# RWKV-7 recurrence: some products on the other two 64x64 tiles, copies moved between engines, and a new order of steps

## What is computed

```python
def _wkv7_scan(S0, r, w, k, v, kk, a):
    def step(S, inp):
        r_t, w_t, k_t, v_t, kk_t, a_t = inp
        sa = jnp.einsum("bhvk,bhk->bhv", S, -kk_t)
        S = (S * w_t[:, :, None, :] + sa[..., None] * (kk_t * a_t)[:, :, None, :]
             + v_t[..., None] * k_t[:, :, None, :])
        o_t = jnp.einsum("bhvk,bhk->bhv", S, r_t)
        return S, o_t
...
    kk = kk / jnp.maximum(jnp.sqrt(jnp.sum(kk * kk, axis=-1, keepdims=True)), 1e-12)
...
    mean = jnp.mean(o, axis=-1, keepdims=True)
    var = jnp.mean(jnp.square(o - mean), axis=-1, keepdims=True)
    o = ((o - mean) * lax.rsqrt(var + LNX_EPS) * lnx_g + lnx_b)
    o = o + jnp.sum(r * k * r_k, axis=-1, keepdims=True) * v
    o = o.reshape(B, T, D) * jax.nn.silu(g)
    return o @ w_o, h[:, -1], S
```

## Time and profile before

| | us |
|---|---|
| median of 3 runs | 1933.91 |
| lowest, highest | 1926.66, 1935.87 |
| the profiled execution | 1932.09 |
| its span, first to last instruction | 1930.1 |
| PE busy | 1802.9 (93%) |
| DVE busy | 1049.6 (54%) |
| ACT busy | 798.0 (41%) |
| POOL busy | 249.6 (13%) |

### The profile page before, as it was taken

One profiled execution on the slowest core, in us unless ns is written; L12 is line 12 of the kernel. 1 busy time (PEld: TensorE's weight loads), 2 busy tenths in 40 slices (PEclk: granted clock), 3 DMA queues, 4 the chain that ended last, 5 costly groups with the idle time before them and its releaser, 6 DMA issues.

```text
span 1930.1 us, 43901 instructions
## 1 busy us (share of the span) xinstructions
PE 1802.9 (93%) x18432; PEld 1538.8 (80%) x18432; DVE 1049.6 (54%) x1718; ACT 798.0 (41%) x1459; POOL 249.6 (13%) x315
## 2 busy tenths in 40 slices
PE   7999999999999999999998998999999998778797
PEld 6988999999888888799986776777776776334697
DVE  6744464453588999444445533443463445676334
ACT  4234233233466767333333323233343444555233
POOL 0300000000245555232000000000000001010032
PEclk9999999999999999999999999999999999998899
DMA  8534554555355553243889999999999999999541
GB/s 295 185 142 156 179 180 155 170 179 165 92 137 139 142 137 97 92 141 143 340 292 417 420 419 409 414 426 425 426 426 417 414 425 380 418 393 364 211 146 71
DMA packets 154200, 510.45 MB, mean 264 GB/s; under 512 B 60097, under 2 KB 81986, under 8 KB 108738
## 3 DMA queue, kind: packets, MB, share of 16 engines
q1 hardware_dynamic: 153442, 503.66, 68.8%
q10 hardware_dynamic: 576, 4.19, 0.6%
HBM read 472.86 MB, written 32.32 MB: 262 GB/s over the span
## 4 chain that ended last, share of the span: by engine, by line
PE 31%; DMA 19%; DVE 3%; ACT 2%; issue 2%; SPq 1%; DVEq 0%; ACTq 0%
DMA at_vraw<-in_cache_v 19%; PE psP L2648 8%; PE psP L2650 7%; PE psP L2649 7%; PE at_psO L2702 5%; PE at_psS L2681 3%; SPq L2061 1%; PE psP L2747 0%; DVE wlo L2410 0%; SPq L2101 0%; PE at_psT L2693 0%; DVE at_w L2498 0%; ACT at_p_w L2368 0%; DVE at_p_rc L2593 0%; ACT at_p_w L2366 0%
## 5 line engine op out<-in xcount | busy, mean ns | idle before, releaser
L2648 PE MATMUL psP<-xhi,whi 128*128 128x320 f32 x1488 | 475.3, 319 | 2.9 <-DVE xlo L2535 1.9
L2650 PE MATMUL psP<-xhi,wlo 128*128 128x320 f32 x1488 | 460.7, 310 | 0.0
L2649 PE MATMUL psP<-xlo,whi 128*128 128x320 f32 x1488 | 460.5, 309 | 0.0
L2648 PEld LDWEIGHTS psP<-xhi,whi 128*128 128x128 f32 x1488 | 280.2, 188 | 64.9 <-issue 63.4
L2410 DVE TENSOR_TENSOR wlo<-wraw,whi 128x2048 fp32r<-128x2048 f32 x92 | 212.9, 2314 | 207.7 <-ACT whi L2236 207.5
L2236 ACT ACTIVATE whi<-wraw 128x2048 fp32r<-128x2048 f32 x92 | 176.0, 1913 | 276.7 <-PE psP L2650 275.5
L2649 PEld LDWEIGHTS psP<-xlo,whi 128*128 128x128 f32 x1488 | 280.5, 189 | 0.1
L2650 PEld LDWEIGHTS psP<-xhi,wlo 128*128 128x128 f32 x1488 | 280.3, 188 | 0.0
L139 PE MATMUL psP<-xhi,whi 128*128 128x320 f32 x704 | 218.1, 310 | 2.7 <-DVE wlo L174 2.3
L140 PE MATMUL psP<-xlo,whi 128*128 128x320 f32 x704 | 217.6, 309 | 0.0
L141 PE MATMUL psP<-xhi,wlo 128*128 128x320 f32 x704 | 217.5, 309 | 0.0
(11 more groups left out here) (382 smaller groups left out, 3075.5 us busy)
## 6 DMA issues: line engine op xcount, KB each, us to landing
wraw<-in_weights SPq DMA_DIRECT2D x156, 1024.0 KB, 5.9
at_kraw<-in_cache_k SPq DMA_DIRECT2D x96, 1024.0 KB, 11.1
at_vraw<-in_cache_v SPq DMA_DIRECT2D x94, 1024.0 KB, 10.9
at_kraw<-in_cache_k SPq DMA_DIRECT2D x64, 512.0 KB, 9.8
at_vraw<-in_cache_v SPq DMA_DIRECT2D x62, 512.0 KB, 10.7
rw_s0t<-in_s0T SPq DMA_DIRECT2D x16, 256.0 KB, 3.7
o_wkv_s<-rw_SN SPq DMA_DIRECT2D x16, 256.0 KB, 3.1
wraw<-in_weights ACTq DMA_DIRECT2D x4, 1024.0 KB, 6.5
```

What stands on the lines that cost most here:

```text
L2648: pe.matmul(out, wh, c_.xhi[:, kc, :], start=(kc == 0), stop=False)
L2649: pe.matmul(out, wh, c_.xlo[:, kc, :], start=False, stop=False)
L2650: last = pe.matmul(out, wl, c_.xhi[:, kc, :], start=False, stop=(kc == NM - 1))
```

## The change

Three products move to the two cross tiles: `ss`, `var`, and in `AB` the products with KZ. A cross tile takes rows of one head and writes to the partitions of the other, so `sq` and `csq` are written with their halves exchanged (two ACT instructions of 64 partitions each in place of one of 128; the sum brings the halves back), and `KK` is read from PSUM with exchanged halves (two DVE instructions of 64 partitions). The copies of SA0 to SA3 go from DVE to ACT, and xl from DVE to POOL. `ORDER` is a new list. The semaphore of the moved blocks is split in two, for B and for K, and in every tile `S0` now waits for both; before, it did so only in the last.

```diff
-LATE = set("""... R.g.y R.a.xh R.v.xl P.t.Ht P.a.Ht
+LATE = set("""... R.g.y R.a.xh R.g.xl P.t.Ht P.a.Ht
...
-STILL_READ = {"s4": "v.D4s", "X": "v.X", "S3": "v.ST3", "mean": "v.cen", "O0": "a.O0", "O1": "a.O1", "SN": "v.SNa"}
+STILL_READ = {"s4": "v.D4s", "X": "v.X", "S3": "v.ST3", "SA4": "a.SA4", "O4": "a.O4", "O2": "a.O2"}
...
+                    elif name == "xl":
+                        R.a.wait(pool, "xh", t)
+                        R.g.done(pool.tensor_tensor(c_.xlo[:, t], yv[:], c_.xhi[:, t], ALU.subtract), name)
...
-                        F.a.done(act.activation(sq[:], ins["k"][:], ACT.Square, scale=scalar("k_k", t)), name)
+                        for here, there in (halves, halves[::-1]):
+                            squared = act.activation(sq[there], ins["k"][here], ACT.Square, scale=scalar("k_k", t)[here])
+                        F.a.done(squared, name)
...
-                    elif name[0] == "U":
+                    elif name[0] == "U" or name[0:2] == "SA":
+                        into = {"U4": U4} | {f"U{c}": U for c in range(NCH)} | {f"SA{c}": SA[c] for c in range(NCH)}
                         R.t.wait(act, name, t)
-                        R.a.done(act.activation((U4 if name == "U4" else U)[:], psR[:, banks_r.of(name), 0:HS], ACT.Copy), name)
+                        R.a.done(act.activation(into[name][:], psR[:, banks_r.of(name), 0:HS], ACT.Copy), name)
...
-                        R.a.done(act.activation(csq, cen, ACT.Square), name)
+                        for here, there in (halves, halves[::-1]):
+                            squared = act.activation(csq[there], cen[here], ACT.Square)
+                        R.a.done(squared, name)
...
-                        Q.v.done(dve.tensor_tensor(pair(KK[t % 2][:]), pair(quads[:, ak]),
-                                                   flat(c_.mSI[:]).unsqueeze(1).to_broadcast([P, NCH, 2 * L]), ALU.mult), name)
+                        for h in range(2):
+                            here, there = slice(L * h, L * h + L), slice(L * (1 - h), L * (1 - h) + L)
+                            masked = dve.tensor_tensor(pair(KK[t % 2][here]), pair(quads[there, ak]),
+                                                       flat(c_.mSI[there]).unsqueeze(1).to_broadcast([L, NCH, 2 * L]), ALU.mult)
+                        Q.v.done(masked, name)
...
-            def over_channels(out, mat, x):
-
-                for r in halves:
-                    last = pe.matmul(out[r], mat[r, r], x[r], start=True, stop=True)
+            def over_channels(out, mat, x, exchanged=False):
+
+                for r, to in zip(halves, halves[::-1] if exchanged else halves):
+                    last = pe.matmul(out[to], mat[r, r], x[r], start=True, stop=True)
                 return last
...
-                            for out, lhs in ((ps, zt[0]), (other, zt[1])):
-                                for r in halves:
-                                    last = pe.matmul(out[r, cc], lhs[r, c], flat(ar[r, c]),
+                            for out, lhs, swap in ((ps, zt[0], 0), (other, zt[1], 1)):
+                                for h, r in enumerate(halves):
+                                    last = pe.matmul(out[halves[h ^ swap], cc], lhs[r, c], flat(ar[r, c]),
                                                      start=True, stop=True)
...
                         elif name[0] == "S":
-                            if c == 0 and t == TILES - 1:
-                                pe.wait_ge(turned_in, 128 * (t + 1))
-                            R.v.wait(pe, f"SA{c}", t)
+                            if c == 0:
+                                pe.wait_ge(b_turned, 64 * (t + 1))
+                                pe.wait_ge(k_turned, 64 * (t + 1))
+                            R.a.wait(pe, f"SA{c}", t)
```

More of the change, by code:

```diff
@@ L1062, in flat @@
             return x.rearrange("p c l -> p (c l)")
+        halves = [slice(64 * h, 64 * h + 64) for h in range(2)]
         block = ctx.enter_context(nc.Block())
@@ L1563, in _ @@
             pe.wait_ge(masks, c_.n_masks)
-            halves = [slice(64 * h, 64 * h + 64) for h in range(2)]
             def free_p(name, t):
@@ L1707, in run @@
                     elif name == "O4":
-                        R.a.wait(pe, R.a.last("SA4", "O2"), t)
+                        R.a.wait(pe, "SA4", t)
                         for r in halves:
@@ L1730, in run @@
                         R.a.wait(pe, "csq", t)
[L1731 removed]
+                        R.t.done(over_channels(psR[:, banks_r.of(name), 0:TOK], blkm, csq, exchanged=True), name)
                     else:
```

67 lines of the change are left out of this document (37 added, 30 removed).

## The result

The changed kernel takes 1945.94 us, the median of four runs (1941.17 to 1948.97), beside 1933.26 us for the kernel before: a ratio of 1.0056, with a 95% interval of 1.003 to 1.0082. It is slower by 0.3 to 0.8%, some 12 us, where I had forecast 17 us less. Its profiled execution had 1941.17 us, the fastest of the four, with a span of 1939.4.

A forecast was written before the change was run, and what follows sets the result against it. PE was taken as the bound, DVE and the inverse's chain close behind. From 1932.1 us, -1.3 in each of 14 slots (-18), -1 in partly filled slots and +1 for waits gave 1914, 1916 as median; range 1904 to 1930.

The forecast's parts named there:

- The limit: Recurrence slots of 16.35 us: PE has about 15.6 us of work, with DVE's queue and the inverse's chain next.
- the chain of the inverse: One tile's triangular inverse through PE, ACT and DVE each slot: 16.35 us before, forecast 14.95 in the new order.
- The cross tiles overlap fully: AB's products with K run beside those with B on idle tiles: -0.89 us of PE a slot, lower bound 0.
- rival B: The cross tiles do not overlap; PE keeps 15.6 us, slots stay at 16.1, -4 us, 1930; chance 0.06.
- The price of the halves: sq, csq and KK as two 64-partition instructions, each at full time; DVE gets at most +0.57 us net for KK.
- Z1's: Chain piece from Yt to Z1, with SN and S2 now ahead: 3.5 us in place of 3.11.
- 15.05: Forecast length in us of a full recurrence slot: chain 14.95 plus 0.1 for DVE meeting POOL.
- Rival A: SyncE's DMA queue or a late load of a sets the pace: slots 15.6 to 15.9, 1925 us; chance 0.20.
- Rival C: S0 waits for late moved blocks of B and K: slots 16.7 to 17, +7 us, 1941; chance 0.06.
- Waits for things that are late now and then give about +1: Term in the forecast's sum for occasional late inputs in the recurrence: about +1 us.
- Against: this slot has a weight transfer beside it, which most have not: Argument against SyncE's queue setting the pace: its 15.25 us was counted in a slot with a weight transfer.
- The clock: Sign of a wrong forecast: granted clock at half in more places of the recurrence, since PE rests more; no size given.

The follow-up runs named there:

- e5_straight: e3_both with ss, var and K's part of AB back on the straight tiles, new order kept; 1939.38 us, 1.0024 to the kernel before.
- e3_both: Changed kernel with a's load ahead of B's moves and the weight transfers 3.9 us into slots 4, 6, 8 and 10; 1923.29 us.
- e10_early: Changed kernel with a's load ahead of B's moves and wo's four early weight transfers in slots 1 and 2; 1925.04 us.
- e11_before_early: Kernel before with its four weight transfers in slots 1 and 2, nothing else changed; 1933.74 us.
- e12_early_only: Changed kernel with the weight transfers in slots 1 and 2, a's load left behind B's moves; 1930.84 us.
- e1_a_first: Changed kernel with only the load of a moved ahead of B's four moves on SyncE's queue; 1929.96 us.
- e9_double: e3_both with each of the four 1 MB weight transfers made a second time in the next slot; 1937.85 us.
- e7_split: Changed kernel with a's load ahead, four weight transfers cut into 16 of 256 KB, two in each of slots 4 to 11; 1924.62 us.

## Why the prediction was wrong, point by point

**The limit.** In the undisturbed slots PE, DVE and the chain of the inverse lie close together, as forecast. That the chain sets the length is argued, not shown: its pieces, taken from one last transpose to the next, add up to the slot whatever bounds it. The forecast of each engine's busy time held: DVE 14.2 to 14.4 us (forecast 14.1 to 14.8), ACT 13.1 (13.4), POOL 10.0 to 10.4 (10.3).

**The cross tiles overlap fully, as taken from the earlier trace rows.** In the timeline of PE, the groups of AB, one after the other with B and with K, start 0.02 to 0.09 us apart, and U0's products with KK follow at 740.16, 0.9 us after the first with B (the first with K had started at 739.15, ahead of it). Behind the dots S0 (rw_Kn) and var (stage_a):

```profile
739.25 0.31 PE L1643 MATMUL psP<-rw_AR,rw_BZ 64*64 64x128 f32 x2
739.31 0.28 PE L1643 MATMUL psP<-rw_AR,rw_KZ 64*64 64x128 f32 x2
739.39 0.28 PE L1643 MATMUL psP<-rw_AR,rw_BZ 64*64 64x128 f32 x2
...
740.16 0.28 PE L1699 MATMUL rw_psR<-rw_Vn,rw_KK 64*64 64x64 f32 x4
...
743.57 0.27 PE L1699 MATMUL rw_psR<-rw_Vn,rw_Kn 64*64 64x64 f32 x2
743.60 0.49 PE L1601 MATMUL rw_psR<-stage_a,rw_blkm 64*64 64x320 f32 x2
743.65 0.25 PE L1699 MATMUL rw_psR<-rw_Vn,rw_Kn 64*64 64x64 f32 x2
...
743.92 0.44 PE L1601 MATMUL rw_psR<-stage_a,rw_blkm 64*64 64x320 f32 x2
```

var stands behind S0 in the program, and its first pass starts at 743.60, ahead of S0's second pair at 743.65. By the profile's ends, which are modelled, that pair ends before it; by the starts alone, six records of S0 begin between var's first pass and its second at 743.92. It uses the same rows of the array as S0. The Trainium skill, "TensorE: Matmul & The Clock Gate", section "The mechanism", has products start and end in program order and lets weight loads overlap only in another row group; the starts above show otherwise for the cross tiles, and the measurement decides. My rival B is out. `ss` is overlapped in the same way. Not all of var's share is a gain: U4, next in the queue, waits for ACT's copy of Q4 and starts 0.8 us after var in this kernel (slot 13), where it starts 0.5 after it in e5_straight.

**The price of the halves.** KK's two instructions took 0.69 us each, its full time twice, as I took it.

**The chain was put 0.5 us too short.** Its pieces, by the same starts and ends as before, in an undisturbed slot of e3_both (slot 3):

| piece | before | forecast | measured |
|---|---|---|---|
| to Dt | 3.97 | 2.6 | 2.66 |
| to D2t | 2.29 | 3.0 | 3.13 |
| to Y | 2.24 | 2.3 | 2.09 |
| to Yt | 1.78 | 1.8 | 1.82 |
| to Z1 | 3.11 | 3.5 | 3.87 |
| to X1t | 2.96 | 1.75 | 1.88 |
| sum | 16.35 | 14.95 | 15.45 |

The term that was mis-sized most is Z1's, by 0.37 us. The parts that I listed for it come to 3.31 us and not to the 3.5 that I wrote, so against them 0.56 is missing. Of this 0.26 is a wait: SN waits there for Vnx, which POOL now makes behind SAx and Rz. I had costed SN's products and its change of tile form, but not this wait. In the changed kernel's last full slot (the same 0.26 is in e3_both):

```profile
749.67 0.66 PE L1740 MATMUL rw_psR<-rw_Vnx,rw_Kn 32*64 32x256 f32 x8 [0.26 <-POOL rw_Vnx L1229]
```

With the chain as measured, 15.05 would have been 15.5: 14 slots at -0.85 us are -12 in place of -18. The pair e10_early and e11_before_early, with no late load and no transfer in the full slots, differs by 8.4 us in twelve slots and by 8.7 in the medians.

**Rival A had the right mechanism and the wrong price.** I let a late a cost 0.5 to 0.9 us a slot, as if it landed late by the same amount each time. In e12_early_only it cost less, 0.24 us a slot; in slots 4 and 6 of the changed kernel far more, 2.9 and 2.8 us over 15.5. Missing were the clock behind the wait and what else is under way. From issue to landing a took 2.2 to 5.0 us, by the view by tile of the changed kernel:

```profile
DMA to landing us min/median/max: 2.2/3.1/5.0
```

In the kernel before:

```profile
DMA to landing us min/median/max: 2.2/2.5/4.2
```

The two loads of a that were on their way with the third and fourth weight transfer took 4.7 and 4.9 us, and in the two later profiles of the same kernel 6.3 to 7.1; in all its other full slots a took 2.4 to 4.4.

**Rival C** did not come about in the changed kernel, because the late a held PE first; e1_a_first showed it once a was early.

**The step that failed** is the term "Waits for things that are late now and then give about +1" in the sum, and behind it the sentence "Against: this slot has a weight transfer beside it, which most have not". Over 15.5 us a slot the twelve slots of the changed kernel lost 20.6 us to lateness; the twelve of the kernel before lost 4.4 over its 16.35. I took the transfer's place as given. It is issued by ACT at the place of Vn, and the change moves Vn. I followed a moved step into SyncE's queue, and not to what another engine hangs on the same place in the list. The issue stands in the trace of the kernel before, 3.9 us into slot 8, and took 6.6 us to land:

```profile
641.64 0.33 ACTq L1363 DMA_DIRECT2D wraw<-in_weights  x1
```

With the new list its new place, at the slot's end and over the load of a, could have been worked out beforehand (it came 14.8 to 17.7 us into the slot), and a late a was already the sign of my rival A. In medians the 30 us between forecast and result are 15.1 for the transfers' new place (e12_early_only to the changed kernel), 5.8 for that of a (e10_early to e12_early_only), and 9.0 by which even e10_early stays above 1916, 6 of them the chain's 0.45 us a slot.

**The clock.** I named a clock at half as a sign of failure and gave it no price. It was granted at half for 20.4 us between 548 and 755 in the profile after, against 3.4 us before. Slot 9 shows its share: 3.6 of its 6.2 us are the wait. The other 2.6 I put down to the 6.8 us at 1.2 GHz; no run held the clock apart from the wait.

## What to carry to other kernels

Before a step is moved, look for everything that takes its place from the step's name in the list, on all engines; a transfer that goes along with it can cost more than the step. When a slot is shortened, list what each engine's queue waits for from outside, and leave the loads more room than before, since one that is 4 us late costs 6 with the clock behind it. And work moved to an idle unit pays only if what it takes elsewhere (here DVE's second half of KK) goes to an engine with time left: the same tiles lost 0.3% in one order and won 0.8% in the other.

## What the runs showed of the hardware

A transfer of 1 MB beside a dense stretch can stop PE for up to 4.1 us though PE needs nothing of it there. In e3_both, e9_double and the kernel before, every such stop of 1.3 us or more came just behind a gap of 6.8 to 9.7 us between two blocks of instructions; in e7_split, with 256 KB to a transfer, the four gaps were 6.0 to 6.8 us. Without transfers in the full slots there was no stop of this kind. The dose and the removal show that the transfers cause the stops. That they do it by the late blocks is the reading that fits the gaps, and the 2.2 to 3.0 us from a late block's start to PE's; it wasn't tried apart from the transfers.

Products on the two cross tiles and on the straight ones run side by side though they share rows and partitions: AB took 0.9 us for 1.78 in e5_straight, and between the two passes of a product of 320 columns six records of 64 columns started on the other pair.

An instruction on 64 partitions takes as long as one on 128: 0.69 us for half of KK, 0.65 for the whole.
